# Two transformer blocks on one core: the memory's projection moved from the start into the differential attention

## What is computed

```python
proj = einsum(rmsnorm(x, norm_mix_g), w_in)        # q, k, v and u
q, k = partial_rope(q, positions), partial_rope(k, positions)
a = diff_attention(q, k, v, lam)                   # softmax(c=0) - lam * softmax(c=1), causal
c = u[..., :512] * sigmoid(u[..., 512:])
c = causal_dwconv(c, cv_dw_w) + cv_dw_b            # 31 taps, 4 blocks of 128 channels
h = h + einsum(concat(rmsnorm(a), silu(layernorm(c))), w_out)
kv = einsum(rmsnorm(mem, norm_mem_g), w_ckv)       # the memory's projection: 256 tokens, 2048 columns
h = h + cross_attention(rmsnorm(h, norm_cross_g), kv, ...)
```

## Time and profile before

| | |
|---|---|
| median of 3 runs | 3625.0 us (3619.19 to 3626.53) |
| profiled execution | 3620.42 us, span 3618.2 us |
| PE busy | 3383.9 us (94%) |
| DVE busy | 2204.9 us (61%) |
| POOL busy | 1830.2 us (51%) |
| ACT busy | 750.0 us (21%) |
| the chain that ended last | PE 81%, DVE 14% |

### The profile page before, as it was taken

One profiled execution on the slowest core, in us unless ns is written; L12 is line 12 of the kernel. 1 busy time (PEld: TensorE's weight loads), 2 busy tenths in 40 slices (PEclk: granted clock), 3 DMA queues, 4 the chain that ended last, 5 costly groups with the idle time before them and its releaser, 6 DMA issues.

```text
span 3618.2 us, 41187 instructions
## 1 busy us (share of the span) xinstructions
PE 3383.9 (94%) x16148; PEld 2779.5 (77%) x16148; DVE 2204.9 (61%) x3423; ACT 750.0 (21%) x1188; POOL 1830.2 (51%) x994
## 2 busy tenths in 40 slices
PE   7875889999899999899999999999999999999999
PEld 7653767888687688788877888878888887888887
DVE  1786337992213625777563488879983434787874
ACT  2122222210112612222211111124441111111110
POOL 6430435776343154300165666653436666667665
PEclk9986899999899999999999999999999999999999
DMA  4210212222221022100032333335454334655553
GB/s 172 67 53 0 70 47 77 99 99 94 82 76 58 30 82 76 53 13 13 24 111 90 113 139 140 139 135 195 183 193 161 121 117 145 204 186 186 191 191 107
DMA packets 164223, 391.72 MB, mean 108 GB/s; under 512 B 10688, under 2 KB 69056, under 8 KB 161984
## 3 DMA queue, kind: packets, MB, share of 16 engines
q1 hardware_dynamic: 73648, 264.04, 21.3%
q10 hardware_dynamic: 90384, 125.05, 10.1%
HBM read 326.14 MB, written 62.91 MB: 108 GB/s over the span
## 4 chain that ended last, share of the span: by engine, by line
PE 81%; DVE 14%; ACT 1%; issue 1%; POOL 1%; DMA 1%; ACTq 0%; DVEq 0%; SPq 0%; POOLq 0%
PE bank L1299 23%; PE bank L1301 22%; PE bank L1300 22%; DVE sb_gated L1205 3%; PE bank L337 2%; DVE sb_onehot L1202 2%; PE bank L639 1%; PE bank L354 1%; PE bank L650 1%; PE bank L723 1%; PE bank L647 1%; DVE sb_cacc L1698 1%; DVE sb_tmp L1245 1%; DVE sb_tmp L407 1%; POOL sb_wL L1287 1%
## 5 line engine op out<-in xcount | busy, mean ns | idle before, releaser
L1287 POOL TENSOR_TENSOR sb_wL<-sb_raw,sb_wH 128x1024 fp32r<-128x1024 f32 x495 | 1212.2, 2449 | 1755.1 <-PE bank L1301 1753.1
L1299 PE MATMUL bank<-sb_hH,sb_wH 128*128 128x512 f32 x2504 | 1012.6, 404 | 35.4 <-DVE sb_cpad L1680 15.4
L1300 PE MATMUL bank<-sb_hL,sb_wH 128*128 128x512 f32 x2504 | 987.0, 394 | 0.0
L1301 PE MATMUL bank<-sb_hH,sb_wL 128*128 128x512 f32 x2504 | 986.9, 394 | 0.0
L1282 POOL TENSOR_SCALAR sb_wH<-sb_raw 128x1024 fp32r<-128x1024 f32 x495 | 633.9, 1281 | 16.1 <-DMA sb_raw<-in_weights 16.1
L1299 PEld LDWEIGHTS bank<-sb_hH,sb_wH 128*128 128x128 f32 x2504 | 478.0, 191 | 160.9 <-issue 47.9
L1300 PEld LDWEIGHTS bank<-sb_hL,sb_wH 128*128 128x128 f32 x2504 | 478.5, 191 | 101.0 <-issue 6.9
L1301 PEld LDWEIGHTS bank<-sb_hH,sb_wL 128*128 128x128 f32 x2504 | 477.2, 191 | 102.2
L1299 PE MATMUL bank<-sb_pzH,sb_wH 128*128 128x512 f32 x1024 | 401.7, 392 | 13.5 <-DVE sb_pzL L1249 11.4
L1300 PE MATMUL bank<-sb_pzL,sb_wH 128*128 128x512 f32 x1024 | 399.7, 390 | 0.0
L1301 PE MATMUL bank<-sb_pzH,sb_wL 128*128 128x512 f32 x1024 | 399.5, 390 | 0.0
(11 more groups left out here) (350 smaller groups left out, 4127.9 us busy)
## 6 DMA issues: line engine op xcount, KB each, us to landing
sb_raw<-in_weights SPq DMA_DIRECT2D x495, 512.0 KB, 3.2
gates<-sb_stage ACTq DMA_DIRECT2D x16, 2048.0 KB, 7.7
acts<-sb_sq ACTq DMA_DIRECT2D x96, 256.0 KB, 2.0
sb_Gt<-gates ACTq DMA_DIRECT2D x24, 1024.0 KB, 7.1
sb_Ga<-acts ACTq DMA_DIRECT2D x24, 1024.0 KB, 10.6
sb_Gt<-gates ACTq DMA_DIRECT2D x4, 2048.0 KB, 11.4
sb_xT<-in_xT SPq DMA_DIRECT2D x1, 2048.0 KB, 13.0
acts<-sb_xT ACTq DMA_DIRECT2D x1, 2048.0 KB, 9.6
```

Of the source, the lines that this page charges most:

```text
L1287: nc.gpsimd.tensor_tensor(wL[:, t % LOS, :], raw[:, t % RAWS, :], wH[:, t % HIS, :].bitcast(F32), ALU.subtract).then_inc(sems("weights_lo" ...
L1299: pe.matmul(out, hi, H, start=start, stop=False)
L1300: pe.matmul(out, hi, L, start=False, stop=False)
L1301: return pe.matmul(out, lo, H, start=False, stop=stop)
```

## The change

x is loaded first, in four parts, on SP's queue, and the constants, the parameters and the positions on ACT's; `memT` is loaded behind the first three weight tiles. x is normalized at once, without the memory ahead of it, and `in_u` and `in_qkv` are the first tiles. The memory's norm is cut up: squares and sums beside the first `in_u` tiles, its root on DVE behind 8 taps, its scaled parts behind gate(3). The 16 half tiles `ckv` run one to a unit of the attention, in bank 0, and the transposes of the values, in bank 1, from unit 9 on. For that the scores have banks 2 to 5, two units instead of three, and are made one unit ahead. The products of tiles and their number are the same. The diff, cut to its core:

```diff
@@ -66,7 +66,7 @@
...
 _at = 0
-for _name, _n in (("ckv", 16), ("in_u", 8), ("in_qkv", 12), ("out", 8), ("cq", 8), ("co", 8), ("up", 44),
+for _name, _n in (("in_u", 8), ("in_qkv", 12), ("ckv", 16), ("out", 8), ("cq", 8), ("co", 8), ("up", 44),
                   ("down", 22), ("sb_qkv", 24), ("gate_sb", 8), ("branch_sb", 8), ("ba", 1), ("gdn_qkv", 24),
...
@@ -80,7 +80,8 @@
...
     _z = 0 <= _t - TILE["z"] < 8
-    BANK.append(None if _down else (7, 0)[(_t - TILE["z"]) % 2] if _z else 7 if _gate else (0, 1, 7)[_t % 3] if _conv else _t % 2)
+    _mem = 0 <= _t - TILE["ckv"] < 16
+    BANK.append(None if _down else 0 if _mem else (7, 0)[(_t - TILE["z"]) % 2] if _z else 7 if _gate else (0, 1, 7)[_t % 3] if _conv else _t % 2)
     BEFORE_IN_BANK.append(0 if _down else BANK[:_t].count(BANK[_t]))
...
@@ -224,13 +225,14 @@
...
         B.update(over([("kmem", [P, 8, NMEM], F32), ("vmem", [P, MB, D], F32)], (
-            lambda: over([("memT", [P, 8, NMEM], F32), ("mH", [P, 8, NMEM], F32R), ("mL", [P, 8, NMEM], F32R),
-                          ("vmT", [P, 4, NMEM], F32)]),
             lambda: over([("qkT", [P, 8, S], F32), ("vT", [P, 4, S], F32), ("vtok", [P, TB, S], F32),
-                          ("cpad", [P, 4, S + 32], F32), ("cacc", [P, 4, S], F32), ("cos", [P, S], F32),
-                          ("sin", [P, S], F32), ("pos", [P, S], I32), ("p", [P, 2, 2, S], F32),
-                          ("att", [P, 2, S], F32), ("attT", [P, 2, S], F32), ("oT", [P, 4, S], F32)]),
+                          ("cpad", [P, 4, S + 32], F32), ("cacc", [P, 4, S], F32), ("p", [P, 2, 2, S], F32),
+                          ("att", [P, 2, S], F32), ("attT", [P, 2, S], F32), ("mH", [P, 8, NMEM], F32R),
+                          ("mL", [P, 8, NMEM], F32R)]),
+            lambda: over([("past_qk", [P, 8, S], F32), ("oT", [P, 4, S], F32), ("past_v", [P, TB, S], F32),
+                          ("past_conv", [P, 8, S + 16], F32), ("memT", [P, 8, NMEM], F32)]),
             lambda: over([("qx", [P, 8, S], F32), ("px", [P, 2, NMEM], F32), ("pxT", [P, 2, MB, S], F32)]))))
+        B.update(over([("cos", [P, S], F32), ("sin", [P, S], F32), ("pos", [P, S], I32)]))
         B.update(over([("zH", [P, FFB, S], F32R), ("zL", [P, FFB, S], F32R), ("uab", [P, 2, 2, S + 2], F32)]))
...
@@ -501,6 +508,7 @@
...
                  (0, slice(offs[0], offs[1]), slice(0, qw[0]))]
+        vmT = sq[:].rearrange("p a b -> p (a b)")[:, 0:4 * NMEM].rearrange("p (b m) -> p b m", b=4)
         sb_t = [B["sbt"][:, c, :] for c in range(2)]
...
@@ -1262,12 +1270,12 @@
...
         def _(sp):
-            sp.dma_start(cst[:], a["consts"]).then_inc(sems("consts_in"), 16)
-            sp.dma_start(par[:], a["params"]).then_inc(sems("consts_in"), 16)
-            if first:
-                sp.dma_start(B["memT"][:], a["memT"].rearrange("(k p) t -> p k t", p=P)).then_inc(sems("mem_in"), 16)
-            sp.dma_start(xT[:], a["xT"].rearrange("(k p) t -> p k t", p=P)).then_inc(sems("x_in"), 16)
+            x_blocks = a["xT"].rearrange("(n k p) t -> n p k t", p=P, k=2)
+            for n in range(KB // 2):
+                sp.dma_start(xT[:, 2 * n:2 * n + 2, :], x_blocks[n]).then_inc(sems(f"x_in{n}"), 16)
             for t in range(N_TILES):
+                if first and t == RAWS:
+                    sp.dma_start(B["memT"][:], a["memT"].rearrange("(k p) t -> p k t", p=P)).then_inc(sems("mem_in"), 16)
                 if t >= RAWS:
...
@@ -1338,21 +1346,24 @@
...
-                norm_pe(E, **NORMS["mem"])
-                m_hi, m_lo = (lambda k: B["mH"][:, k, :]), (lambda k: B["mL"][:, k, :])
-                products("ckv", 8, m_hi, m_lo, NMEM, ready=parts_ready)
+                norm_pe(E, **NORMS["mix"])
+                def memory_norm(b, k):
+                    if k == 6:
+                        for g in (2 * b, 2 * b + 1) if b < 4 else ():
+                            sum_block(E, g == 0, nt=MB)
+                        if b == 6:
+                            spread_pe(E, NMEM)
+                def beside_u(b, k):
+                    if b == 0:
+                        parts_ready(k)
+                    memory_norm(b, k)
                 for b in range(8):
-                    t = TILE["ckv"] + 8 + b
-                    one_tile(t, m_hi, m_lo, NMEM)
-                    sum_block(E, b == 0)
-                    emptied(E, t)
-                    E.at("mem_turned", b - 1)
-                    for m in range(MB):
-                        mm = turn(ps[5 + b % 2][:, m * P:(m + 1) * P], B["vmT"][:, b % 4, m * P:(m + 1) * P])
-                    mm.then_inc(sems("mem_turn"), 1)
-                norm_pe(E, summed=True, **NORMS["mix"])
-                E.arrive()
-                products("in_u", 8, h_hi, h_lo, ready=parts_ready)
+                    one_tile(TILE["in_u"] + b, h_hi, h_lo, ready=lambda k: beside_u(b, k))
                 products("in_qkv", 8, h_hi, h_lo)
...
@@ -1377,18 +1388,31 @@
...
                     h, i = units[u]
-                    E.at("probs", 2 * (u - 2))
+                    E.at("probs", 2 * (u - 1))
                     for c in range(2):
                         r = slice(64 * c, 64 * c + 64)
-                        nc.tensor.matmul(ps[2 * (u % 3) + c][:, 0:P * (i + 1)],
+                        nc.tensor.matmul(ps[2 + 2 * (u % 2) + c][:, 0:P * (i + 1)],
                                                   B["qkT"][r, h, i * P:(i + 1) * P],
...
+                m_hi, m_lo = (lambda k: B["mH"][:, k, :]), (lambda k: B["mL"][:, k, :])
+                def turn_memory(w):
+                    emptied(E, TILE["ckv"] + 8 + w)
+                    E.at("mem_turned", w)
+                    for m in range(MB):
+                        mm = turn(ps[1][:, m * P:(m + 1) * P], vmT[:, w % 4, m * P:(m + 1) * P])
+                    mm.then_inc(sems("mem_turn"), 1)
                 scores(0)
-                scores(1)
                 for u in range(len(units) + 1):
-                    if u + 2 < len(units):
-                        scores(u + 2)
+                    if u + 1 < len(units):
+                        scores(u + 1)
+                    if u < len(units):
+                        one_tile(TILE["ckv"] + u, m_hi, m_lo, NMEM, ready=None if u else parts_ready)
+                    if u >= 9:
+                        turn_memory(u - 9)
                     if u < len(units):
...
@@ -1502,34 +1530,29 @@
...
                 act.activation(sc[:, 2:4], sc[:, 0:2], ACT.Exp).then_inc(sems("lam_exp"), 1)
+                norm_act(E, when=lambda k: eng.wait_ge(sems(f"x_in{k // 2}"), 16), **NORMS["mix"])
                 eng.wait_ge(sems("mem_in"), 16)
-                norm_act(E, **NORMS["mem"])
-                copy_tiles("ckv", 8, lambda b: B["kmem"][:, b, :], NMEM)
-                eng.wait_ge(sems("x_in"), 16)
-                for b in range(8):
-                    square(E, xT[:, b, :])
-                    if b >= 4:
-                        E.at("mem_turn", b - 3)
-                    t = TILE["ckv"] + 8 + b
-                    tile_ready(E, t)
-                    empties(act.activation(B["vmT"][:, b % 4, :], bank(t, NMEM), ACT.Copy), t)
-                norm_act(E, squared=True, **NORMS["mix"])
-                E.meet()
-                eng.dma_start(B["pos"][:], a["pos"].partition_broadcast(P)).then_inc(sems("pos_in"), 16)
+                for k in range(4):
+                    square(E, B["memT"][:, k, :], NMEM)
                 E.wait("angles")
...
                 for b in range(4):
+                    if b == 2:
+                        root_act(E, MB)
                     t = TILE["in_u"] + 2 * b + 1
...
                     empties(act.activation(tmp[:, b, :], bank(t), ACT.Sigmoid), t)
+                    for k in range(4, 8) if b == 0 else ():
+                        square(E, B["memT"][:, k, :], NMEM)
+                for k in range(KB):
+                    hi_part(E, B["mH"][:, k, :], NMEM)
                 copy_tiles("in_qkv", 8, lambda b: B["qkT"][:, b, :])
...
                     act.activation(B["vtok"][:, :, b * P:(b + 1) * P],
-                                            ps[5 + b % 2][:, :].rearrange("p (t d) -> p t d", t=TB), ACT.Copy).then_inc(sems("v_copied"), 1)
+                                            ps[(6, 2)[b % 2]][:, :].rearrange("p (t d) -> p t d", t=TB), ACT.Copy).then_inc(sems("v_copied"), 1)
                 E.meet()
...
@@ -1546,6 +1569,9 @@
...
                         probabilities(u + 1)
+                    if u >= 12:
+                        E.eng.wait_ge(sems("mem_turn"), u - 11)
+                    copy_tiles("ckv", 1, lambda _: B["kmem"][:, u, :] if u < 8 else vmT[:, u % 4, :], NMEM, at=u)
                     E.wait("att_turned")
...
@@ -1645,15 +1671,8 @@
...
                 chain(v.tensor_scalar(sc[:, 6:7], sc[:, 3:4], sc[:, 2:3], -0.2, ALU.subtract, ALU.add))
-                eng.wait_ge(sems("mem_in"), 16)
-                norm_dve(E, chain, **NORMS["mem"])
-                for b in range(8):
```

(30 more changed lines are left out.)

13 lines of the change are left out of this document (8 added, 5 removed).

## The result

| | before | after |
|---|---|---|
| median of the runs, us | 3619.35 (6 runs, 3614.42 to 3626.53) | 3636.34 (6 runs, 3620.93 to 3643.45) |
| profiled execution, us | 3620.42 | 3624.32 |
| its span, us | 3618.2 | 3621.9 |
| mean granted clock of TensorE | 0.962 | 0.966 |

The ratio is 1.004 (95%: 1.0023 to 1.0056): the kernel is slower by 17 us, and by more than 0.2%. With the further runs the median of before is 3619.35, and the difference is +17.

The account below looks back on a forecast made before the run. Limits differed by stage: POOL and PE while the memory is projected, PE from 156.3 to 236.2 us, DVE in the attention units. Start -69 plus units +79 gave +10; on the 3625.0 median, 3635 us, range 3595 to 3660.

Parts of the forecast that it names:

- The start: From kernel start to the first attention unit: x normalized before the memory gains time, -69 us (bounds -72 and -62).
- the sums of squares cost 32 matmuls in 6.96 us: Start, PE: summing x's squares takes 32 matmuls, 6.96 us at the low clock, ending near 19.4 us.
- The memory's norm: Spread over the input tiles: sums in tiles 2 and 3 cost 0.9 us, its spread 0.5, a late rotation 0.5.
- The cover ahead of the rotation: DVE's 11.15 us wait before the rotation hides the memory's products and low parts, 9 to 11 us; nearly all goes.
- The wait for the scores: Attention units: with scores one unit ahead, DVE waits for PE before its maxima, 2.2 us a unit (bounds 1.7 and 3.1).
- POOL's lock: Attention units: POOL's weight splits block DVE's taps or weight steps through shared SBUF ports, 2.5 us a unit (bounds 0 and 2.9).
- wrong if the taps stay at 0.74, no lock: Sign in the units: DVE's taps should average near 1.1 us; staying at 0.74 would mean POOL does not block DVE.
- rival a: Units: half tile ends after +7, POOL misses DVE's sensitive steps; total -30 us, 3595 us; chance 0.22 faster, 0.13 level.
- Copies of turned values: Units: eight DVE copies of the memory's values from PSUM at 0.42 us, the last two behind the last unit; 4 us.
- behind the units nothing changes: After the attention units: no change counted; a warmer PE there could give 2 us, left out.
- Rival b: Units: PE idles some 4 us per unit and restarts at the low clock; total +31 us, 3656 us; chance 0.15.
- Rival c: Start: loads share the DMA engines, all landing at 16.2 us instead of 11.5; total +15 us, 3640 us; chance 0.05.

## Why the prediction was right, and where its steps were off

**The start: -60.4 us where -69 was predicted.** Most of the miss is one term. Timeline of the changed kernel's start:

```profile
11.65 13.79 PE L344 MATMUL bank<-sb_consts,sb_sq 128*128 128x1 f32 x64 [11.65 <-ACT sb_sq L290]
...
27.01 0.69 DVE L392 TENSOR_TENSOR sb_dg<-sb_consts,bank 128x512 f32<-128x512 f32 x1
27.75 2.08 PE L361 MATMUL bank<-sb_dg,sb_consts 128*128 128x512 f32 x2 [2.32 <-DVE sb_dg L392]
...
32.15 0.77 PE L1307 MATMUL bank<-sb_hH,sb_wH 128*128 128x512 f32 x1 [2.32 <-DVE sb_hL L463]
...
49.12 2.60 POOL L1295 TENSOR_TENSOR sb_wL<-sb_raw,sb_wH 128x1024 fp32r<-128x1024 f32 x1 [2.51 <-PE bank L1309]
49.55 2.45 DVE L1691 TENSOR_SCALAR sb_cos<-sb_cos 128x512 f32<-128x512 f32 x1
...
53.13 0.76 PE L1307 MATMUL bank<-sb_hH,sb_wH 128*128 128x512 f32 x1 [4.16 <-DVE sb_cpad L1699]
```

The step "the sums of squares cost 32 matmuls in 6.96 us" is the mis-sized term. The row of 10.33 in the earlier trace rows is of the memory's 256 columns; x has 512. I scaled the spread, which stands in the next sentence, from 256 to 512 columns, and not the sums. They are 64 records in 13.79 us, 6.8 more, at the same 0.22 each. The number in the row invites the error: the trace has two records for each of these small matmuls, so its x32 are the memory's 16, although 32 is also what the program issues for x (4 a block, 8 blocks). The prediction called this pace that of the low clock; the view of the stretch gives a granted clock of 1.00 (11.65 to 25.44 us), while later sums take 0.12 us a record (59.55, below). Which level it is stays open; the sum doesn't hang on it. The squares began at 10.89 instead of 11.8, so the diagonal came at 27.01 instead of 21.0: 6.0 late. The spread is 2.08 (2.1 predicted). The norm ended at 40.35 instead of 34.4, still 6.0 late.

From there to the third input tile it took 12.8 us instead of 11.3. Three angle steps from 42.17 on last 4.98 us (2.15 before), and the row of 49.55 lasts 2.45 (0.43 before), each beside a split of POOL: 4.9 us. The 11.3 us taken from the earlier trace rows held such delays too, on other steps:

```profile
105.90 2.35 POOL L1287 TENSOR_TENSOR sb_wL<-sb_raw,sb_wH 128x1024 fp32r<-128x1024 f32 x1 [2.04 <-PE bank L1301]
106.08 2.44 DVE L1663 TENSOR_SCALAR sb_att<-sb_att 128x512 f32<-128x512 f32 x1
108.56 1.15 DVE L1664 TENSOR_SCALAR sb_att<-sb_att 128x512 f32<-128x512 f32 x1
```

These two take 0.43 us each in the changed kernel, so 2.7 us of delay stood in the old chain and 4.9 stand in the new one, 2.1 more. The prediction took the chain over whole and had not asked which splits of POOL fall into it. With these the tile stands at 53.13 instead of 45.7, 7.4 late; the test that I had set ("wrong if the first product comes after 30 us") was met, at 32.15.

The memory's norm cost the rest: from the third tile to the first mask it is 176.73 - 53.13 = 123.6 us, and it was 237.13 - 116.41 = 120.7, so +2.9 where 1.9 was predicted. The sums in tiles 2 and 3 account for the difference: 0.9 us predicted, and 0.94 + 0.95 measured, twice 8 records where the text had 8 in all, the same count as at the start:

```profile
59.55 0.94 PE L344 MATMUL bank<-sb_consts,sb_sq 128*128 128x1 f32 x8
```

The cover ahead of the rotation held. DVE still idled 4.49 us there, where I had it nearly used up:

```profile
102.12 2.38 DVE L463 TENSOR_TENSOR sb_mL<-sb_tmp,sb_mH 128x256 fp32r<-128x256 f32 x1 [0.15 <-ACT sb_mH L457]
...
143.32 0.69 DVE L1742 TENSOR_TENSOR sb_tmp<-bank,sb_sin 128x512 f32<-128x512 f32 x1 [4.49 <-PE bank L1373]
```

The products and low parts ran from 95.69 to 104.43, 8.7 us with one delay by POOL (102.12), just under the 9 to 11 costed.

**The wait for the scores: 2.4 us a unit where 2.2 was predicted.** 39.1 us in 15 waits, the first of them the 1.1 of before, released by PE's scores as the text said. The granted clock was 0.79, not 0.75, so the mean between the warm and the cold end was near, if a little low. Shown: with the wait taken away (scores two ahead) 35.0 us go by the medians and 37.9 between the marks.

**POOL's lock: 2.4 us a unit where 2.5 was predicted, but on other instructions.** I had said the taps would show it, with a mean near 1.1 us; they stayed at 0.74. By my own sign ("wrong if the taps stay at 0.74, no lock") the lock would have been absent, and it was not: the weight steps carry it. The sign was wrong, and not the timing under it, which left both places open ("within the taps or the weights"): the half tile took 4.6 us on PE (187.71 to 192.3), between the 2.9 and 5.8 us that I had for the two clock levels, started only when the scores had ended, and ended some 6.6 us behind the steps of `att` (+5.3 to +7 in the text), so POOL fell on the steps behind the taps every time. The price is the same since it is POOL's duration and not DVE's:

```profile
182.18 2.34 POOL L1295 TENSOR_TENSOR sb_wL<-sb_raw,sb_wH 128x1024 fp32r<-128x1024 f32 x1 [9.07 <-PE bank L1309]
182.26 2.34 DVE L1776 TENSOR_SCALAR sb_att<-sb_p,sb_ss 128x128 f32<-128x128 f32 x1
184.48 1.05 POOL L1290 TENSOR_SCALAR sb_wH<-sb_raw 128x1024 fp32r<-128x1024 f32 x1
184.63 1.03 DVE L1777 SCALAR_TENSOR_TENSOR sb_att<-sb_p,sb_ss,sb_att 128x128 f32<-128x128 f32 x1
...
221.56 2.81 POOL L1295 TENSOR_TENSOR sb_wL<-sb_raw,sb_wH 128x1024 fp32r<-128x1024 f32 x1 [4.32 <-PE bank L1309]
...
222.28 2.10 DVE L1774 TENSOR_TENSOR sb_ss<-sb_ss,sb_sc 128x1 f32<-128x1 f32 x1
224.34 1.04 POOL L1290 TENSOR_SCALAR sb_wH<-sb_raw 128x1024 fp32r<-128x1024 f32 x1
224.41 1.04 DVE L1776 TENSOR_SCALAR sb_att<-sb_p,sb_ss 128x128 f32<-128x128 f32 x1
```

A DVE step on one element a partition, 0.16 us alone, lasts 2.10 (222.28). So an early and a late half tile cost alike as long as a step of this kind comes within POOL's time; the bound "0" (rival a, the lock misses) needed the tile to end behind the weights, and PE's transposes wait for the weights. Rival a is out. In the Trainium skill ("SBUF — State Buffer", section "Who interferes with whom") it is said that issue order, not the shape of the operation, decides who blocks; these rows agree, 2.10 us for one element. The same section of the Trainium skill names `tensor_scalar` among the operations that can take the shared ports, though it has one input, when its operands meet certain conditions. The rows of 182.26 and 49.55 agree: they are such `tensor_scalar` steps, at 2.34 and 2.45 us, and my text spoke of steps with two operands in SBUF only.

**Copies of turned values: 4 us predicted, 6.0 measured**, 3.3 of copies and 2.7 of waits for PE ahead of the last two. But "behind the units nothing changes" was off the other way: DVE waits 5.06 us for the last product with v where it waited 10.88, and the stretch up to the second mark is 4.9 us shorter. The units alone lost 82.3 us (164.1 instead of 81.8), and that the total came to 77.4, so near to 79, is in part because these two errors cancel.

**The rivals.** Rival b (cold and full) put both terms at their upper ends; the clock of 0.79 spoke against it. The other signs came too: POOL was 56.5 us busy in the units (55 predicted), and the units ended near 341, 164 us after they began (158 predicted). Rival c (DMA sharing) had x and the constants late: the constants were in at 8.54 us, where 9.2 was predicted, and the squares began at 10.89, where 11.8 was; so it is out too.

**The sum.** -60.4 + 77.4 = +17.0 at the second mark, and +17.0 by the medians. The start was 8.6 us worse than predicted and the rest 1.6 better, +7 in all, and 3635 met 3636.34 because the median that it was added to stood 5.7 higher in three runs than it does in six. That is luck: with the median of six runs the same sum gives 3629. That both sums read 17.0 is luck too, since the six runs of the changed kernel lie 22.5 us apart. What the prediction had right is the mechanism, two losses of some 2.4 us a unit against a gain at the start, and with it the direction. By the two profiled executions alone the change would cost 3.9 us. What lies between is in unchanged stages, and here is one stretch of them, with the granted clock as the number ahead of the last two, in the changed kernel's first and second profile:

```profile
1240.00:1270.00 30.00, 25.96 (x106) 17.71 (x105) 21.65 (x49) 18.54 (x25) 3.55 (x2) 1.00 0.05 18
```

```profile
1240.00:1270.00 30.00, 25.95 (x99) 18.16 (x98) 20.27 (x45) 19.83 (x27) 3.56 (x2) 0.92 0.06 18
```

The same program was granted 1.00 in one execution and 0.92 in the other near the same place, and its two profiled spans are 15.2 us apart (3621.9 and 3637.1), though at the second mark they differed by 1.0. That the clock of such stretches makes the spread is argued from these rows, not shown by an experiment; it stays open. The verdict rests on the medians.

## What to carry to other kernels

Work that is moved beside an engine's full stage costs that engine what the *helpers* of the work do to it: here PE had the room, and POOL's 3.4 us a weight tile (with 2.4 us of it landing on DVE) and the shorter lead of the scores were the bill, 74 us for 63 us of hidden work. When a buffer is given up, count how many units the producer still runs ahead, and what stands ahead of it in program order; here one reordering (scores two ahead), with no bank given back, turned +15 us into -20 by the medians on one chip. And when a duration is taken from a row, read the width of its tile and scale every term by it, not only the one that is in mind.

## What the runs showed of the hardware that was not expected

- POOL's delay of DVE hardly depends on which steps it meets: 37.7 us, all on the weight steps, in the changed kernel; 38.1 us on taps and weight steps with scores two ahead; 36.6 with the squares added as well.
- A `tensor_scalar` of one tensor operand is held as well (2.34 us instead of 0.29, at 182.26).
- DVE gets one instruction in between two of POOL's: at 224.34 POOL starts its second step while DVE's held step ends at 224.38, and the next one, issued at 224.41, lasts 1.04 us, again POOL's duration.
- An ACT instruction on the same weight tile is not held (1.05 us at 206.14 beside POOL's 206.00 to 208.52, and 1.05 in all 16 of them), and moving the high part there gave 14 us between the marks.
- The sums over one column cost 0.22 us a record at the start (64 in 13.79 us, 8 in 1.84) and 0.12 beside the input tiles (8 in 0.94), and each small matmul shows as two records.
